# Strip sums of three feed-forward stages built in HBM by accumulating transfers, spread over the stage before

## What is computed

```python
def half_swiglu(x, g, w_up, w_down):
    h = rms_norm(x, g)
    a, b = jnp.split(h @ w_up, 2, axis=-1)
    return x + 0.5 * ((jax.nn.silu(a) * b) @ w_down)
```

## Time and profile before

| | |
|---|---|
| time, median of three runs | 2734.53 us |
| span of the profiled execution, first to last instruction | 2732.7 us |
| TensorE busy | 2707.3 us (99%) |
| VectorE busy | 1729.2 us (63%) |
| ScalarE busy | 1103.5 us (40%) |
| POOL busy | 999.8 us (37%) |
| transferred | 238.04 MB, 87 GB/s on average |

### The profile page before, as it was taken

The page is one execution under the profiler, slowest core; times in us unless marked ns, Lnnn a source line. Parts: engine busy times, 40 slices in busy tenths (PEclk is TensorE's granted clock), DMA queues, the critical chain, the costliest instruction groups (busy, mean ns, idle before and its releaser), DMA issues. The chain is left out here.

```text
span 2732.7 us, 46951 instructions
## 1 busy us (share of the span) xinstructions
PE 2707.3 (99%) x18804; PEld 2646.4 (97%) x18804; DVE 1729.2 (63%) x2801; ACT 1103.5 (40%) x1858; POOL 999.8 (37%) x610
## 2 busy tenths in 40 slices
PE   9999999999999999999999999999999999999998
PEld 8999999998999999999999999999989999999997
DVE  8747576887433693838685647668773347837475
ACT  5324244636322352424443333454463224424242
POOL 2333333345433333333333333333544333333332
PEclk9999999999999999999999999999999999999999
DMA  3222222233122222222222222222332222222222
GB/s 118 99 71 93 77 87 93 88 124 125 63 71 91 75 73 84 78 93 78 94 77 85 70 95 78 92 86 88 132 109 70 77 88 74 75 79 78 93 78 85
DMA packets 72853, 238.04 MB, mean 87 GB/s; under 512 B 8304, under 2 KB 17264, under 8 KB 72176
## 3 DMA queue, kind: packets, MB, share of 16 engines
q1 hardware_dynamic: 57888, 208.30, 22.1%
q10 hardware_dynamic: 14800, 27.51, 2.9%
HBM read 227.52 MB, written 8.27 MB: 86 GB/s over the span
## 5 line engine op out<-in xcount | busy, mean ns | idle before, releaser
L498 POOL TENSOR_TENSOR w_lo<-w_raw,w_hi 128x1024 fp32r<-128x1024 f32 (+1 forms) x254 | 600.0, 2365 | 962.8 <-ACT w_hi L1131 947.7
L1131 ACT ACTIVATE w_hi<-w_raw 128x1024 fp32r<-128x1024 f32 (+1 forms) x238 | 250.2, 1051 | 796.1 <-PE lin L635 660.8
L635 PE MATMUL lin<-h_hi,w_hi 128*128 128x320 f32 x1600 | 373.8, 315 | 2.9 <-DVE tmp L1614 2.7
L635 PE MATMUL lin<-h_hi,w_lo 128*128 128x320 f32 x1600 | 364.6, 309 | 0.0
L635 PE MATMUL lin<-h_lo,w_hi 128*128 128x320 f32 x1600 | 364.1, 309 | 0.0
L635 PE MATMUL lin<-g_hi,w_lo 128*128 128x320 f32 x1408 | 320.9, 309 | 0.0
L635 PE MATMUL lin<-g_lo,w_hi 128*128 128x320 f32 x1408 | 320.8, 309 | 0.0
L635 PE MATMUL lin<-g_hi,w_hi 128*128 128x320 f32 x1408 | 320.7, 309 | 0.0
L550 POOL TENSOR_TENSOR lo_A<-raw_even,hi_A 128x512 fp32r<-128x512 f32 x120 | 167.8, 1398 | 376.3 <-ACT hi_A L1185 376.3
L635 PEld LDWEIGHTS lin<-h_hi,w_hi 128*128 128x128 f32 x1600 | 265.2, 188 | 15.9 <-issue 11.3
L635 PEld LDWEIGHTS lin<-h_lo,w_hi 128*128 128x128 f32 x1600 | 267.5, 188 | 0.0
(11 more groups left out here) (334 smaller groups left out, 6215.6 us busy)
## 6 DMA issues: line engine op xcount, KB each, us to landing
w_raw<-wts SPq DMA_DIRECT2D x240, 512.0 KB, 3.5
raw_even<-wts SPq DMA_DIRECT2D x88, 512.0 KB, 4.4
raw_odd<-wts SPq DMA_DIRECT2D x64, 512.0 KB, 4.2
caches<-kcache_in ACTq DMA_DIRECT2D x16, 512.0 KB, 4.0
caches<-vcache_in ACTq DMA_DIRECT2D x16, 512.0 KB, 4.7
x<-x_in SPq DMA_DIRECT2D x8, 320.0 KB, 6.6
k_out<-kT ACTq DMA_DIRECT2D x2, 1280.0 KB, 4.6
v_out<-v_sb ACTq DMA_DIRECT2D x2, 1280.0 KB, 8.6
```

What stands on the lines that cost most here:

```text
L498: ins = nc.gpsimd.tensor_tensor(w_lo[:, s, cols], w_raw[:, s, cols], w_hi[:, s, cols].bitcast(F), ALU.subtract)
L635: ins = nc.tensor.matmul(out[:, half, :], w, a[:, half * HALF:(half + 1) * HALF], start=first and n == 0, stop=last and n == 2)
L1131: nc.scalar.activation(w_hi[:, s, 0:cols], w_raw[:, s, 0:cols], ACT.Copy).then_inc(hi_ready.sem, 1)
```

## The change

For stages 2, 3 and 4 (of four; `from_dram`) the sums are no longer made by VectorE. During the stage before, they are built in an internal HBM tensor `made` of 3 x 19 x 4 strips. SP opens each sum with a copy of one strip inside HBM (`open_sums`), and POOL adds the other strip with an accumulating transfer (`add_sums`), S2 from S1, S4 from S2. Both go by slots: one slot per pair and one per output tile, 43 in a stage; the sums of pair k are opened in slots 2k (S1, S3) and 2k + 1 (S2, S4), and added in slots 2k + 1 (S1, S3), 2k + 2 (S2) and 2k + 4 (S4). In the stage that uses them, SP loads S1, S2 and S4 with a transfer each (`load_sum`) and S3 as the third strip of the raw pair. Since a transfer can only add, the scheme's signs are changed: the strips are all added, and the tokens' sums and VectorE's later steps subtract instead. The first stage makes its sums on VectorE as before.

```diff
+        made = nc.dram_tensor("strip_sums", (2 * DEPTH - 1, NP, 4, P, 4 * P), F, kind="Internal").ap()
...
             def pair_free(L, q):
 
                 sp.wait_ge(strip_ready["S3"].sem, strip_ready["S3"].count(L, q + 1))
-                sp.wait_ge(sums_done["S4"].sem, sums_done["S4"].count(L, q + 1))
+                if from_dram(L, q):
+                    sp.wait_ge(strip_ready["A11"].sem, strip_ready["A11"].count(L, q + 1))
+                    sp.wait_ge(strip_ready["A12"].sem, strip_ready["A12"].count(L, q + 1))
+                else:
+                    sp.wait_ge(sums_done["S4"].sem, sums_done["S4"].count(L, q + 1))
                 sp.wait_ge(strip_ready["A22"].sem, strip_ready["A22"].count(L, q + 1))
 
             def load_pair(L, q, i, weight):
...
+                if from_dram(L, q):
+                    sp.wait_ge(sum_added["S3"], 16 * ((2 * L - 1) * NP + q + 1))
+                    sp.dma_start(raw_[:, 0:2, :].rearrange("p a n -> p (a n)"), wts[n]).then_inc(sem, 16)
+                    sp.dma_start(raw_[:, 2, :], made[2 * L + q // NP - 1, q % NP, 2]).then_inc(sem, 16)
+                    sp.dma_start(raw_[:, 3, :], wts[n + 1][:, 4 * P:]).then_inc(sem, 16)
...
+            def load_sum(L, q, i, name, early=False):
...
+                if name == "S1":
+                    sp.wait_ge(strip_ready["S1"].sem, strip_ready["S1"].count(L, q))
+                    to = S1_sum
+                elif name == "S2":
+                    sp.wait_ge(strip_ready["S4"].sem, strip_ready["S4"].count(L, q if i == 0 else q - 1))
+                    to = S2_sum[i % 2]
...
+                else:
+                    sp.wait_ge(strip_ready["S2"].sem, strip_ready["S2"].count(L, q + 1))
+                    to = S2_sum[i % 2]
+                sp.wait_ge(sum_added[name], 16 * ((2 * L - 1) * NP + q + 1))
...
+            def open_sums(L, f, slot):
...
+                for name, src in (("S2", wts[n][:, 0:4 * P]), ("S4", wts[n][:, 4 * P:])) if second else (
+                        ("S1", wts[n + 1][:, 0:4 * P]), ("S3", wts[n][:, 0:4 * P])):
+                    sp.wait_ge(sum_opened[name], 16 * ((fi - 1) * NP + k))
+                    sp.dma_start(made[fi - 1, k, SUMS.index(name)], src).then_inc(sum_opened[name], 16)
...
-                    for i in range(pairs):
+                    for i in range(pairs + 2):
                         if i == 1:
                             sp.wait_ge(lo_ready.sem, lo_ready.count(L, n))
-                        if i:
+                            if g == 0 and from_dram(L, q):
+                                sp.wait_ge(evacuated.sem, evacuated.count(L, (0, FFN2_RES)[f] + 2 * PLAIN))
+                        if 2 <= i and (g or i > 2):
+                            load_sum(L, q + i - 2, i - 2, "S4")
+                        if 2 <= i <= pairs:
+                            load_sum(L, q + i - 1, i - 1, "S1")
+                        if 1 <= i < pairs:
                             load_pair(L, q + i, i, w + 2 * i)
+                            load_sum(L, q + i, i, "S2")
+                        if i < pairs:
+                            open_sums(L, f, next(slots))
...
-                        if j == 1 and g == len(SEGMENTS) - 1 and f and L < DEPTH - 1:
+                        if j == 3 and g == len(SEGMENTS) - 1 and f and L < DEPTH - 1:
                             pair_free(L, q + pairs - 1)
-                            load_pair(L + 1, 0, 0, 2 * PLAIN)
+                            load_first(L + 1, 0)
...
+            def add_sums(L, f, slot):
...
+                for name, at_, other in (("S1", 1, None), ("S3", 1, None), ("S2", 2, "S1"), ("S4", 4, "S2")):
...
+                    pool.wait_ge(sum_opened[name], 16 * (done + 1))
+                    pool.wait_ge(sum_added[name], 16 * done)
+                    if other:
+                        pool.wait_ge(sum_added[other], 16 * (done + 1))
...
+                    nc.gpsimd.dma_start(made[fi - 1, k, SUMS.index(name)], src,
+                                        accum_op=ALU.add, max_dma_last_dim=4096).then_inc(sum_added[name], 16)
...
             def add_strips(L, q, i, name):
 
+                if from_dram(L, q):
+                    return
...
-                nc.vector.tensor_tensor(u2[i % 2], middle[i % 2], u1[i % 2], ALU.add).then_inc(u2_kept.sem, 1)
+                nc.vector.tensor_tensor(u2[i % 2], u1[i % 2], middle[i % 2], ALU.subtract).then_inc(u2_kept.sem, 1)
```

More of the change, by code:

```diff
@@ L407, in pairs_landed, with raw_count, from_dram, sum_landed @@
             per_ffn = sum((n + 1 - side) // 2 for n in SEGMENTS)
-            before = sum((n + 1 - side) // 2 for n in SEGMENTS[:g])
-            return pair_in[side].sem, pair_in[side].count(L, 32 * (f * per_ffn + before + i // 2 + 1))
+            nth = sum((n + 1 - side) // 2 for n in SEGMENTS[:g]) + i // 2 + 1
+            back = per_ffn * (2 * L + f - 1)
+            return side, nth, back, per_ffn
+        def raw_count(L, q):
+            side, nth, back, per_ffn = pairs_landed(L, q)
+            return pair_in[side], 32 * nth if back < 0 else 32 * per_ffn + 48 * (back + nth)
+        def from_dram(L, q):
+            return L > 0 or q >= NP
+        def sum_landed(L, q, name):
+            side, nth, back, _ = pairs_landed(L, q)
+            if name == "S1":
+                return S1_in, 16 * ((2 * L - 1) * NP + q + 1)
+            if name == "S3":
+                return raw_count(L, q)
+            return {"S2": S2_in, "S4": S4_in}[name][side], 16 * (back + nth)
+        def pair_weight(fi, k):
+            L, f = divmod(fi, 2)
+            g = max(g for g in range(len(SEGMENTS)) if FIRST_PAIR[g] <= k)
+            return L * WEIGHTS + f * (FFN_WEIGHTS + MIX_TILES) + 2 * PLAIN + 2 * k + KB * g
+        BUILD_SLOTS = NP + KB * len(GROUPS)
+        assert BUILD_SLOTS >= 2 * NP + 3
         block = ctx.enter_context(nc.Block())
@@ L442, in load_pair @@
                     pair_free(L, q - 2)
[L443 to L446, removed]
+                sem, _ = raw_count(L, q)
+                raw_, n = raw_pair[i % 2], L * WEIGHTS + weight
+                if from_dram(L, q):
[4 more added lines that the diff above has]
+                else:
+                    for j in range(2):
+                        sp.dma_start(raw_[:, 2 * j:2 * j + 2, :].rearrange("p a n -> p (a n)"), wts[n + j]).then_inc(sem, 16)
@@ L568, in ffn @@
                             low_strip(L, q + i + 1, i + 1, "A12")
+                        add_sums(L, f, next(slots))
                     for k in range(KB):
                         low(L, n + k)
+                        add_sums(L, f, next(slots))
                     n, q = n + KB, q + pairs
```

79 lines of the change are left out of this document (62 added, 17 removed).

## The result

The changed kernel takes **2741.28 us** (median of 12 runs, 2735.70 to 2743.28); the kernel before, timed beside it, 2734.52 us (12 runs, 2734.11 to 2735.08). The ratio is 1.0023, with a 95% interval of 1.0014 to 1.0032: slower by 6.8 us. That is past what I had called "no change" (5.5 us) and 1.3 us above that outcome's own range of 2732 to 2740, though inside the forecast's whole range of 2731 to 2800. The spread is a result too: the kernel before lies within 1 us, the changed one within 7.6, with two runs at 2735.7 and 2735.8 and ten from 2740.4 up.

A forecast was written before the change was run, and what follows sets the result against it. TensorE, busy 2707.3 of 2732.7 us, was taken as the bound. With 0 removed, 0 added on TensorE, 0 from POOL and 0.5 us from first groups, 2734.53 became 2735 us; range 2731 to 2800.

The forecast's parts named there:

- rival A: Transfer engines fill up, weight tiles and S4 come late, TensorE waits: mostly near 2768 us, up to 2905; chance 0.30.
- rival B: POOL's issue costs over 2.03 us, so the next w_lo is late in every tile: 2771 us at 2.41; chance 0.13.
- a wait at the first pair of a stage: Listed, with a fixed time before the first or behind the last instruction, as a sign of being wrong otherwise; no size.
- Rival C: VectorE's relief gains something through earlier ends at changes of stage: at most 3 us, 2732 us; chance 0.02.
- The limit of 2.03: Microseconds per POOL issue up to which two fit in each seven-block output tile, with 2.5 us spare spread over eight tiles.
- Waits on POOL: Additions waiting for earlier ones ahead of w_lo in POOL's queue: landings may reach about 9.6 us, so counted 0.
- Two issues at 1.4 are 2.8 us: they fit: In seven-block output tiles of 6.16 us, POOL idles 3.67 to 3.83 us after w_lo, enough for two issues: cost 0.
- the low end: Transfer prices per 256 KB: 0.76 us a copy, 1.52 an addition, so 6.1 of 6.16 us in a seven-block tile: free.
- a share below 1 in tiles: Sign of being right: transfers' share of the engines near 45% on average and below 100% in output tiles.
- the tightest chain: In a pair, S4 may land 13.0 us after SP starts issuing at 1250.82; 11.1 us needed, fitting by 1.9.
- the estimate of 7.6 us a tile: Transfer time per output tile at 1.22 us a copy and about 1.84 an addition, giving about 2770 us.
- The wait moved to first use: In first groups SP loads pair 1 after the sixth plain tile's evacuation: 7.1 of 8.8 us, 0 to 2 us, taken as 0.5.

The follow-up runs named there:

- the kernel with copies alone: Changed kernel with only SP's copies that open the sums left: no POOL additions, VectorE's sums used in all stages; 2734.49 us, ratio 1.0001.
- the use alone: Changed kernel without building: stages 2 to 4 load the sums from slices of the weights, computing other values; 2735.24 us, ratio 1.0004.
- experiments 1 to 4: Follow-ups: parts of the change alone (2734.49 to 2746.70 us), pair 1's loads earlier (2739.96), POOL's additions moved (2738.15 to 2743.62), 18 additions (2781.03 held back, 2734.45 not).
- building alone: Changed kernel with sums built in HBM by copies and POOL additions but never read, VectorE's sums used in all stages; 2746.70 us, ratio 1.0043.

## Why the prediction was right or wrong

- **The forecast as a whole, inside its range by luck.** The middle of it, 2735 us, and the outcome that had a chance of 0.55 missed: the loss of 6.8 us is clear of noise. The whole range reached to 2800 only for the costs of rivals A and B, and of those no more than 0.2 us came. What came was named in one clause, "a wait at the first pair of a stage", and for the larger part not at all.
- **The bound, right but for 0.8 us.** TensorE set the time, and of VectorE's 195 us less nearly nothing comes back. I had counted 0 because the list of waits names none for it; the three waits for acc of about 0.26 us were below what the list shows. Rival C (chance 0.02) was right in kind.
- **Prices on POOL, right and not what mattered.** I took 1.4 us for an accumulating issue; the two groups have means of 1.00 and 0.91 us. The limit of 2.03 was not touched, rival B did not come.
- **Waits on POOL, right as a sum and wrong as an end of the argument.** I counted 0 for them. POOL waits 23.2 us for copies in 15 waits, and in the changed kernel no w_lo is late for it. But a wait of 0.85 us moved two issues right ahead of a w_lo. That is the step that failed: "Two issues at 1.4 are 2.8 us: they fit" compared durations on one engine. It did not ask what VectorE does meanwhile. Its g_lo reads two operands in the on-chip memory beside POOL's w_lo, and the trace of before already showed that one stands for the other: g_lo 1.44 or 2.52 us beside w_lo and 0.82 elsewhere, always ending 0.7 us behind the w_lo. I had not read these rows. Cost: 3.4 us in the profiled execution. The Trainium skill ("SBUF — State Buffer", section "Who interferes with whom") says that a VectorE instruction with two inputs there contends with a GpSimd instruction that reads there, over a pair of ports that is an exclusive lock. The trace agrees, on who contends and on the lock, by the 252 ends of g_lo. What the runs add is that behind an issue g_lo stands not for one w_lo but for two.
- **Transfers, prices right at the low end, and fuller than I said.** 59.78 MB in 12.5% of 2738.7 us are 1.50 us for an addition of 256 KB (I had 1.52). The first queue has 104.6 MB and 327 us more than before (34.0% and 22.1% of the two spans); with 171 loads at 0.76 the 228 copies cost about 0.86 us each (0.76 to 1.52). The kernel with copies alone gives 0.83, from 29.0% of 2732.3 us. These are times of packets, and where the share is above 1 they overlap, so the prices may be too high. The measured prices give 1.52 + 2 x 0.86 + 2 x 1.50 = 6.2 us for a tile of 6.16, and the share of 1.04 over 36 us of tiles says the same: I had named a share below 1 in tiles as a sign of being right, and it was not. Two of rival A's signs came too: ScalarE waits 40.6 us for loads of built sums, and weight loads of stages 2 and 3 land after up to 8.2 us (w_raw) and 10.6 us (raw_even). The slack carried nearly all of it: outside the first pairs it cost TensorE the 0.2 us near 1122 us, where a built sum came later than the "It fits, by 1.9 us" of the tightest chain allowed. As a cost of tens of microseconds rival A, which had 0.30, is out, and with it the estimate of 7.6 us a tile from the two pages of the Trainium skill.
- **The wait moved to first use, right in kind, wrong in size.** I had "It fits by 1.7 us, three times; if not, about 1 us each" and took 0.5 in sum; it was 0.99, 0.40 and 0.81. The term: the loads were counted from the start of the products, but SP issues them 1.7 to 2.5 us later (983.27 to 984.13 against 981.59), and they land in 5.4 us. 2.5 + 5.4 + 2.0 = 9.9 of 8.8 us. Stage 4, where nothing is built, waits 0.81 us, and the use alone 1.5 in sum, so it is the order on SP first; what makes the three differ from run to run is open.
- **The sum.** 3.4 + 2.2 + 0.2 = 5.8 of the 6.0 us between the two spans. Compared matmul by matmul, the start of TensorE's work slips by 3.6, 1.15, 0.4, 0.6 and 1.0 us at these five waits and regains 0.8 at VectorE's three: 5.9.

What stays open. Which runs have the long g_lo is not seen outside the profiles. The two runs at 2735.7 lie 1.2 us over before, about the second loss alone, and those above 2740.4 fit one wait of 3 to 4 us with or without a fall of the clock (it stayed at 1.00 behind the wait of the profiled run and fell behind those of experiments 1 to 4; the mean granted clock is 0.998 in the profiled run and 0.996 or 0.997 in five others of the twelve). That is argued, not shown. Nor was it tried whether a POOL transfer that does not accumulate does the same. Why building alone is slower than building with use is only described: two long g_lo at another place, behind later copies.

## What to carry to other kernels

Before work goes on an engine's queue, look at what another engine does in the same microseconds, above all VectorE operations on two on-chip operands beside POOL's: read whether an operation takes longer in one place than in another (1.44 against 0.82 us), and at whose end it ends, since that marks a shared resource which the new work can tip over. Keep POOL's transfer issues away from a POOL operation that stands ready behind them, or leave a few tenths of a microsecond in which POOL is idle. A wait on SP that protects one buffer belongs directly ahead of the load into that buffer, not ahead of the loads that others need.

## What the hardware showed that I had not expected

- VectorE's two-operand g_lo never finished beside POOL's running w_lo: all 252 that started beside one ended 0.68 to 0.73 us after a w_lo's end, and took up to 2.52 us in the ordinary case against 0.82 alone.
- Accumulating issues on POOL directly ahead of a w_lo hold g_lo until 0.7 us after POOL's second w_lo: 5.3 to 6.7 us, 16 times of 16; with 0.36 us or more between them it never happened. VectorE's operation just ahead of g_lo, with one operand in the accumulators' memory (acc, 118.14 us), took its usual 0.49 us beside the first w_lo.
- At each such wait of TensorE in the experiments (3.0 to 4.4 us, 15 times), its granted clock fell to 0.50 at or near the end of the wait, which cost about 1.7 us more, and 3.4 at two of them. At the 3.4 us wait of the changed kernel it stayed at 1.00.
- Copies within HBM took about 0.83 to 0.86 us of packet time on all transfer engines per 256 KB, and an addition 1.50 us. With a share of 0.80 over 395 us and 1.04 over 36 us, the tiles w_raw landed in 4.1 us instead of 3.5, and no matmul of an output tile waited for one.
